# Down weights of the expert loop on ScalarE's DMA queue instead of SyncE's

## The reference

```python
def hierarchical_moe(x, ...):        # 32 experts: top-1 of 4 groups, then top-2 of 8
    ...
    xs = xt[slot_tok].reshape(n_blocks, MOE_BLOCK, D)
    def expert_block(args):
        xb, e = args
        h = jax.nn.silu(xb @ w_gate[e]) * (xb @ w_up[e])      # 1024 -> 512, twice
        return h @ w_down[e]                                  # 512 -> 1024
    ys = lax.map(expert_block, (xs, blk_expert)).reshape(n_slots, D)
    out = jax.ops.segment_sum(ys * slot_w[:, None], slot_tok, num_segments=n)
```

## Time and profile before

| | |
|---|---|
| median of 3 runs | 2444.55 us (2440.29 to 2451.59) |
| the profiled execution | 2438.25 us, of which the span of its instructions is 2436.1 us |
| busy: PE, DVE, ACT, POOL | 2222.6, 841.7, 468.2, 343.0 us |
| all PE products through line 825 that read ring and arena | 1303.4 us busy, 38.5 us idle before them, 15.0 us of it until a G load |
| DMA read from HBM and written | 510.16 MB and 41.45 MB |
| weight loads, each 2048 KB | 130 of gate and up, 65 of down, all issued by SyncE |

### The profile page before, as it was taken

One profiled execution on the slowest core, in us unless ns is written; L12 is line 12 of the kernel. 1 busy time (PEld: TensorE's weight loads), 2 busy tenths in 40 slices (PEclk: granted clock), 3 DMA queues, 4 the chain that ended last, 5 costly groups with the idle time before them and its releaser, 6 DMA issues. The chain is left out here.

```text
span 2436.1 us, 37961 instructions
## 1 busy us (share of the span) xinstructions
PE 2222.6 (91%) x15351; PEld 1184.0 (49%) x15351; DVE 841.7 (35%) x1791; ACT 468.2 (19%) x943; POOL 343.0 (14%) x401
## 2 busy tenths in 40 slices
PE   8999998886999999998797999989689999999964
PEld 4665757553444444444443556665444444444422
DVE  2133324634121212122825767642422212121216
ACT  0030304221010101011333444431201101010011
POOL 0000000141111111131600000003211111111305
PEclk9999998987999999999897999999689999999997
DMA  9022104344999999997310000010469999999945
GB/s 352 1 76 98 40 1 142 141 184 165 396 391 388 394 386 389 389 387 274 119 52 7 3 5 1 1 70 35 200 224 395 388 400 384 386 378 391 375 158 207
DMA packets 98871, 534.47 MB, mean 219 GB/s; under 512 B 23040, under 2 KB 46880, under 8 KB 73824
## 3 DMA queue, kind: packets, MB, share of 16 engines
q1 hardware_dynamic: 80672, 491.28, 51.8%
q0 software_dynamic: 18112, 41.99, 4.8%
HBM read 510.16 MB, written 41.45 MB: 226 GB/s over the span
## 5 line engine op out<-in xcount | busy, mean ns | idle before, releaser
L825 PE MATMUL banks<-ring,arena 128*32 128x256 f32 (+3 forms) x9952 | 1303.4, 461 | 38.5 <-DMA ring<-in_exp_w_gu 15.0
L825 PEld LDWEIGHTS banks<-ring,arena 128*32 128x32 f32 (+2 forms) x9952 | 536.4, 124 | 746.3 <-issue 608.7
L825 PE MATMUL banks<-ring 128*128 128x512 f32 (+2 forms) x976 | 372.2, 531 | 10.7 <-ACT ring L1468 7.1
L825 PEld LDWEIGHTS banks<-ring 128*128 128x128 f32 (+1 forms) x976 | 183.9, 194 | 156.6 <-issue 139.8
L1830 DVE TENSOR_TENSOR arena<-arena,banks 128x384 f32<-128x384 f32 x65 | 36.0, 554 | 609.7 <-ACT arena L1392 609.7
L761 POOL DMA_INDIRECT expert_out<-arena,scatter_idx x64 | 61.1, 955 | 824.4 <-DVE arena L1839 804.4
L1392 ACT ACTIVATE arena<-banks 128x384 f32<-128x384 f32 x65 | 31.9, 490 | 735.8 <-PE banks L825 735.8
L825 PE MATMUL banks<-arena 128*64 128x128 f32 (+5 forms) x1664 | 157.8, 303 | 16.7 <-DMA arena<-in_mem_w_kv 9.6
L825 PEld LDWEIGHTS banks<-arena 128*64 128x64 f32 (+3 forms) x1664 | 139.0, 169 | 50.2 <-issue 38.0
L718 POOL TENSOR_TENSOR arena<-arena,ln_gb 128x1024 f32<-128x1024 f32 x28 | 69.5, 2482 | 626.5 <-ACT arena L1357 626.5
L1836 DVE COPY arena<-banks 32x256 f32<-32x256 f32 x132 | 56.2, 425 | 280.1 <-PE banks L825 279.2
(11 more groups left out here) (176 smaller groups left out, 1575.7 us busy)
## 6 DMA issues: line engine op xcount, KB each, us to landing
ring<-in_exp_w_gu SPq DMA_DIRECT2D x130, 2048.0 KB, 17.2
ring<-in_exp_w_down SPq DMA_DIRECT2D x65, 2048.0 KB, 21.8
ring<-in_x_t SPq DMA_DIRECT2D x6, 2304.0 KB, 16.4
moe_in<-arena POOLq DMA_DIRECT2D x16, 512.0 KB, 3.0
arena<-expert_out SPq DMA_DIRECT2D x16, 512.0 KB, 4.3
ring<-expert_out SPq DMA_DIRECT2D x16, 512.0 KB, 4.4
ring<-in_a_w_in SPq DMA_DIRECT2D x6, 1024.0 KB, 17.3
arena<-in_a_w_in SPq DMA_DIRECT2D x4, 1024.0 KB, 14.0
```

Source lines behind the costliest of these rows:

```text
L825: return nc.tensor.matmul(out, lhsT, rhs, start=start, stop=stop)
```

## The change

The loads of D(e) for experts 2 to 31 of both layers leave SyncE's queue. ScalarE issues them, each right behind its copies of the results of expert e-2 (`rows_out(e - 2)`), whose wait on `down_ps` covers the slot. D(0) and D(1), the overflow step's loads and all of G stay where they were. No computation, slot, semaphore or count is changed.

```diff
-                def down(e, b):
-                    sp.wait_ge(down_ps, NE * l + e - 1)
-                    part(e, b, 2)
-
...
                 with sp.Fori(0, NE // 2 - 2) as i:
                     for b in range(2):
                         gate_up(2 * i + 3 + b, 1 - b)
-                        down(2 * i + 2 + b, b)
                 gate_up(NE - 1, 1)
-                down(NE - 2, 0)
-                down(NE - 1, 1)
...
                     for b in range(2):
                         silu_of(2 * i + 1 + b)
                         rows_out(2 * i + b, b, r0 + i)
+                        slot = part_slot(b, 2)
+                        act.dma_start(part_rows(slot), part_src(l, 2, 2 * i + b + 2)).then_inc(ring_in[slot], 16)
```

## The result

The changed kernel takes 2463.45 us (median of 9 runs, 2456.09 to 2475.21), the kernel before in the same comparison 2441.31 us (9 runs). The ratio is 1.0094, with a 95% interval of 1.0076 to 1.0112. The forecast was 2454 us, 9.8 us slower, with 2448 to 2461 as its own range and 2440 to 2474 as the wide one. The measured time lies in the wide range and outside the forecast's own.

The account below looks back on a forecast made before the run. Prediction: both later expert stretches are bound by DMA bytes, G arriving just late. Only the delivery order cost, 4.9 us per layer, all other terms 0: 2444.55 + 9.8 = 2454.4 us; own range 2448 to 2461, wide 2440 to 2474.

Parts of the forecast that it names:

- Its own sign for being wrong: In the expert phases, a bounded period above 17.8 or below 17.4 us would show the forecast wrong; 17.6 and 17.7 expected.
- PE's waits for G: In the expert phases, TensorE's waits for gate and up weights would rise from 15 to about 25 us in all.
- SyncE loses 60 issues, ScalarE gains 60: In the expert loops, D issues at 0.33 us each on SyncE, some 0.4 on ScalarE, fall into idle time: 0 us.
- Each D load is issued 1.4 us later: Behind ScalarE's copies, D's issue moves from 845.95 to about 847.3, with its deadline 28 us on: 0 us.
- D no longer stands behind G: one D transfer per layer: In the expert phases, D shares the engines with G, so every G arrives 4.9 us later once per layer: 9.8 us.
- The start of the waits: In layer 0, TensorE's waits for G would begin some five experts earlier, near 744 us, not after 823.
- Efficiency of three queues: Where D and G overlap, 429 GB/s was taken to hold: no loss; the bounds were −17.3 and 116 us.
- Rival B: Where D and G overlap, interleaving costs bandwidth: a 3% loss is 12 us on top of 9.8, 2466 us; chance 0.23.
- Rival C: In the expert phases, G lands as before because GpSimd's packets get fewer turns: nothing changes, 2445 us; chance 0.13.
- rival D: In the gather's slow stretch, two queues raise the rate, period 16.9 to 17.0 us, time 2427 us; chance 0.14.
- Weights moved by arbitration: Each DMA engine goes round its queues packet by packet, so D and G share; at equal shares D takes 9.8 us.

Follow-up runs that it names:

- e1: Kernel before, all loads on SyncE's queue, with D(e+1) issued between the two parts of G(e+2): 2452.00 us against 2440.24, ratio 1.0045.
- h4: Changed kernel with half of the gate and up products and all gathers and scatters left out: period 14.69 us in both layers.
- h1: Kernel before with half of the gate and up products left out, gathers and scatters kept: period 17.65 us in layer 0, 17.70 in layer 1.
- h2: Changed kernel with half of the gate and up products left out, gathers and scatters kept: period 17.88 us in layer 0, 17.97 in layer 1.
- e2: Changed kernel with D(e+1) issued by ScalarE some 13 us later, behind the next silu instead of the copies: ratio 1.0057 to the kernel before.
- h3: Kernel before with half of the gate and up products and all gathers and scatters left out: period 14.78 us in both layers.
- h6: Kernel before with half of the gate and up products and the scatters left out, gathers kept: period 16.89 us in layer 0, 16.76 in layer 1.
- h5: Kernel before with half of the gate and up products and the gathers left out, scatters kept: period 15.59 us in both layers.
- e5: Changed kernel, TensorE waiting for G's second part only ahead of the fifth of eight wide steps: 2452.02 us against 2441.08 for the kernel before, ratio 1.0066.

## Why the prediction came out as it did

The measured 2463.45 us lies in the wide range by the width that was kept for a loss that the sum took at nothing, not by the mechanism. It lies outside the forecast's own range, and 22.9 us is more than the 12.2 us up to which the prediction said "the same"; "slower" had 0.30. Its own sign for being wrong, a bounded period above 17.8 us, came true with 18.07 and 18.12. PE's waits for G rose to 43.3 us, not 25.

*SyncE loses 60 issues, ScalarE gains 60.* Right: 0.34 us each, and ScalarE's idle time before its silus is still 10.4 to 12.1 us.

*Each D load is issued 1.4 us later.* Wrong, without effect: it is issued at 927.90, 0.19 us after the first of the copies, which run from 927.71 to 929.04; before it was 0.12 us.

*D no longer stands behind G: one D transfer per layer.* Right in kind and size: 9.8 us forecast, 11.0 (6.6 to 15.4) measured alone in e1, 4.1 and 5.5 us left in the two layers of the changed kernel after the longer periods are taken off. D landed after 15.1 us and not 10 to 12, though it had half of the rate; between its issue at 927.90 and 931.00 its queue moved nothing.

*The start of the waits.* Forecast near 744 us, measured at 688. The five experts didn't fit the sum even as it stood: five periods with 0.51 us of waiting each are 2.6 us, not 4.9. Eight are 4.1 us. e1, with no third queue, starts there as well in layer 0, so this seems to belong to the order.

*Efficiency of three queues: "I take no loss".* This is the step that failed. The place that it argued from was right: large packets of two queues interleave at full rate (428 GB/s in h4, 426 in the overlap of the changed kernel). But the loss was looked for in the overlap of D and G, and the 332 GB/s of the earlier trace rows were set aside as a matter of small packets. It is the stretch of the gather in which the rate falls, and with a third queue this stretch ends some two us later. The term measures 12 us, give or take 6, as the difference of the changed kernel and e1, and 11 us by the periods of h1 and h2, where 0 was taken and −17 to 116 was the bound. Rival B had the sum (a loss of 3%, 2466 us) with the wrong place for it. Rival C falls with the waits that begin earlier, and rival D with periods that never came under 17.06 us.

*Weights moved by arbitration.* The Trainium skill's rule ("DMA: Bandwidth & Descriptors", "Queues, rings and completion order"), turns from queue to queue on each engine, agrees with this trace: 1.92 against 1.67 MB in nine us, and 13.1 us for the scatter in place of 9.6.

Open: the changed kernel without scatters was not run, so how the 12 us divide between scatter bytes pushed into the gather's stretch and fewer turns of the gather itself is not settled. e2 speaks for the first as the larger, but weakly, since its order term is another. Why a gather slows large packets and a scatter does not is open too.

## What to carry to other kernels

Where DMA sets the pace, a load is early or late only against its deadline: moving a load that has slack ahead of one that has none cost about its transfer time once per bounded phase here, and moving a deadline back by 3.5 us gained about as much. A second queue of large loads gave no rate here (428 GB/s with one and with two), but small transfers landed later beside it; ask which small transfer gets late by it and what that one does to the rest. Read GB/s, not the busy share, to find the stretches where the engines are slow.

## What the runs showed of the hardware

- Two queues of 2 MB loads move 428 GB/s together, one alone also 428 (h4, h3).
- A row gather from HBM of 0.26 MB costs 2.1 us of DMA time per expert, a scatter of as much 0.8 us (h6, h5). In the kernel before, the total falls from 429 to 332 GB/s at a busy share of 0.99 while the gather moves.
- After waits of 1.66, 2.07 and 2.19 us PE's granted clock over 6 us was 0.72 in e1 and e5, with 1.00 in the stretches around, and those experts took 20.5 to 21.2 us in place of 17 to 18. In e2 waits of up to 2.0 us passed without such a fall, so the wait alone doesn't tell.
- A load issued from ScalarE's queue does not wait for the copies ahead of it: its issue (927.90) lies inside them (927.71 to 929.04).
